# Taking the unread matrix products out of the norms' and the experts' waits

## The chip, the cores and the metric

The kernel runs on one core of one Trainium2 chip. The metric is the device time of one execution in microseconds (us). A core has a matrix engine (TensorE, PE in the rows, whose weight loads are shown apart as PEld), a vector engine (VectorE, DVE), a scalar engine (ScalarE, ACT), GpSimd (POOL) and SyncE (SP), which issues the loads. Each runs its own instruction stream, and they wait for each other through semaphores. Matrix products go into eight accumulator banks (PSUM). The profile also tells which share of TensorE's full clock was granted: 1.00 is 2.4 GHz and 0.50 is 1.2 GHz.

## The reference

Three transformer blocks in fp32 on x of 256 rows by 1024 columns. Cut to its structure:

```python
def reference(x, ...):
    # first block
    x = x + hybrid_mixer(rmsnorm(x), ...)                       # gated delta rule and mLSTM
    x = x + memory_cross_attention(rmsnorm(x), rmsnorm(mem), ...)
    x = x + peer_ffn(rmsnorm(x), ...)                           # 16384 experts, top 16 of each head
    h = rmsnorm(x, norm_final_w)
    # second block; post_norm(h, y) = layer_norm(DN_ALPHA * h + y)
    h = post_norm(h, 0.5 * swiglu(h, ...))                      # norm 0
    h = post_norm(h, chunked_sgu_mixer(h, ...))                 # norm 1
    h = post_norm(h, 0.5 * swiglu(h, ...))                      # norm 2
    shared = nsa_shared_kv(h, ...)
    h = post_norm(h, 0.5 * swiglu(h, ...))                      # norm 3
    h = post_norm(h, nsa_mixer(h, shared, ...))                 # norm 4
    return post_norm(h, 0.5 * swiglu(h, ...))                   # norm 5
```

## The kernel before

The 256 rows of x lie in two tiles of 128 rows, `k.x[:, 0, :]` and `k.x[:, 1, :]`. A product needs x with its columns on the partitions, so after each norm TensorE turns both tiles with eight 128x128 transposes each (`turn_chunks`, the transposes are line L575). ScalarE then takes the high part of each bank of four transposes (`split_high`, L404) and VectorE the low part (`split_low`, L409), since every large product is made of three passes, high by high, high by low and low by high (L398, L399, L400, and L3080, L3081 in the gated feed-forward). Weights stream through a ring of slots; ScalarE takes their high part (L247, L301) and VectorE their low part (L256, L307). The stages follow each other in the order of the program. Stages inside one `joined_stages` have no barrier between them; where one such group ends, all engines meet (lines L464 and L479 in the rows).

At the end of a stage that ends in a norm, the last products of tile 0 finish first, then those of tile 1. While TensorE still works on tile 1, VectorE and ScalarE normalise tile 0, and TensorE turns it as soon as its products are out (`norm.tensor`). Then tile 1 must be normalised: VectorE adds the banks to x, ScalarE squares and takes the root, VectorE takes the reciprocal (L2907, L2619, L2724) and scales the two halves (L2911, L2623, L2728), and TensorE turns tile 1, either at once (`last`) or as the first thing of the next stage (`turn_last`, called from `high_first`). In this interval TensorE has no product of the model to make. It runs `stand_in` there: n products of the identity by a constant into a bank that is not read. Its products are line L584. There are eight such places:

| place | where | products in `stand_in` | what comes next on TensorE |
|---|---|---|---|
| 1 | norm after the mixer (`RmsNorm`) | 4 + 6 + 4 | turning tile 1 in the joined stage |
| 2 | norm after the memory attention (`RmsNorm`) | 4 + 6 + 4 | a barrier, then turning tile 1 |
| 3 | the experts' end (`pick_and_run_experts`) | 12, turning tile 0, 8 | a barrier, then turning tile 1 |
| 4 | norm 0 (`PostNorm`) | 3 | the first product of the next stage, by tile 0 alone |
| 5 | norm 1 (`PostNorm`, `last`) | 3 + 7 + 4 | turning tile 1, then a barrier |
| 6 | norm 2 (`PostNorm`) | 3 + 7 + 4 | turning tile 1 in the joined stage |
| 7 | norm 3 (`PostNorm`, `last`) | 3 + 7 + 4 | turning tile 1, then a barrier |
| 8 | norm 4 (`PostNorm`) | 3 + 7 + 4 | turning tile 1 in the joined stage |

Between the portions TensorE waits for VectorE's sum or mean of tile 1 (`added`, `negated`) and for ScalarE's root of it (`rooted`). `turn_chunks` has its own wait for the normalised halves (`normed`). Norm 5 has no `stand_in`.

Of the kernel before, what the change touches and what calls it, by code (L numbers as in the profile page):

```python
# [27 lines left out]
P = 128  # L28
D = 1024
SEQ = 256  # L30
TILES = SEQ // P
# [536 lines left out]
def turn_chunks(pe, k, src, tile, ready, first=0, normed=None, own=range(8)):  # L568

    for c in own:
        if normed is not None and c % 4 == 0:
            pe.wait_ge(normed, 2 * tile + c // 4 + 1)
        ins = pe.transpose(k.psum[:, first + 2 * tile + c // 4, c % 4 * P:(c % 4 + 1) * P], src[:, c * P:(c + 1) * P],  # L575
                           k.ident[:, :])
        if c % 4 == 3:
            ins.then_inc(ready, 1)


def stand_in(pe, k, n, bank=1):

    for _ in range(n):
        pe.matmul(k.psum[:, bank, 0:P], k.ident[:, :], k.ones[:, :], start=True, stop=True)  # L584


def first_norm(k, ctx, begun, xn, gain):
# [1618 lines left out]
def pick_and_run_experts(k, room):  # L2206
# [8 lines left out]
    with ExitStack() as ctx, k.stage() as block:  # L2215
# [37 lines left out]
        def _(pe):  # L2253
# [97 lines left out]
            for i in range(TILES):  # L2351
                for m in (KEYS - 2, KEYS - 1):
                    pe.wait_ge(w_low, m + 1)
                    for half in range(2):
                        pe.wait_ge(tiles.low_done, 2 * (KEYS + m) + half + 1)
                        ins = v_tile(m, half, i)
                ins.then_inc(v_done, 1)
            stand_in(pe, k, 12, 7)
            turn_chunks(pe, k, k.x[:, 0, :], 0, banks, 4, normed)
            stand_in(pe, k, 8, 7)  # L2360

        @block.scalar
        def _(act):
# [294 lines left out]
class PostNorm:  # L2658
# [104 lines left out]
    def tensor(self, pe):  # L2763
        if self.begin:
            turn_chunks(pe, self.k, self.k.x[:, 0, :], 0, self.banks, 4, self.normed)
            stand_in(pe, self.k, 3)
            if self.which != 0:
                pe.wait_ge(self.negated, 2 * TILES)
                stand_in(pe, self.k, 7)
                pe.wait_ge(self.rooted, 2)  # L2770
                stand_in(pe, self.k, 4)
            if self.last:
                self.turn_last(pe, range(DC))

# [96 lines left out]
class RmsNorm:  # L2871
# [72 lines left out]

    def tensor(self, pe):
        turn_chunks(pe, self.k, self.rows[0], 0, self.banks, 4, self.normed)
        stand_in(pe, self.k, 4)
        pe.wait_ge(self.added, 2)
        stand_in(pe, self.k, 6)
        pe.wait_ge(self.rooted, 2)  # L2950
        stand_in(pe, self.k, 4)

    def ends(self):

# [1223 lines left out]
```

## Time and profile before

| what | value |
|---|---|
| time, median of 3 runs | 2253.13 us (2252.58 to 2254.63) |
| the profiled execution's own time | 2254.57 us |
| its span, first to last instruction | 2252.0 us |
| TensorE busy | 2198.6 us, 98% of the span |
| VectorE busy | 1585.8 us, 70% |
| ScalarE busy | 1170.2 us, 52% |
| mean granted clock of TensorE | 0.994 |
| products of `stand_in` | 107 |

The profiled execution has 2.57 us outside its span. Busy time of TensorE is modelled at its ends, so 98% says that it has nearly always something in hand, not that it runs at its peak.

### The profile page before, as it was taken

The page shows a single profiled execution, that of the slowest core. Times are in us where ns is not written, and L with a number is a line of the kernel's source. Part 1 is how long each engine was busy: PE and PEld are TensorE (multiplying, and loading weights), DVE is VectorE, ACT ScalarE, POOL GpSimd, SP SyncE. Part 2 cuts the span into 40 slices and gives each one's busy share as a digit, 9 for nine tenths or more (in the row PEclk, how much of TensorE's full clock was granted, in tenths as well). Part 3 has the DMA queues.
Part 4 walks back from the last instruction along what each step waited for, and adds up shares of the span by engine and source line. Part 5 has one row for each costly group of instructions (what it writes and reads, how often), then busy time and mean ns, then how long its engine had stood idle before and what let it go on. Part 6 is the DMA issues. An engine that isn't in the chain of part 4 may idle for free. (4 is left out here: it accounts for less than half of the span.)

```text
span 2252.0 us, 37012 instructions
## 1 busy us (share of the span) xinstructions
PE 2198.6 (98%) x14606; PEld 1964.1 (87%) x14606; DVE 1585.8 (70%) x2838; ACT 1170.2 (52%) x2007; POOL 38.1 (2%) x21
## 2 busy tenths in 40 slices
PE   7989999999999999999999999999999999999998
PEld 7977889999999998888888889988889788878887
DVE  7975659998889976666666657765657565786655
ACT  6543444555554455565555545544544554585444
POOL 0101000110000000000000000000000000000000
PEclk9999999999999999999999999999999999999999
DMA  7418424555444456656656556536555655404552
GB/s 272 150 45 187 169 86 162 175 175 173 147 146 149 144 170 193 195 192 193 195 183 218 180 195 234 197 127 225 174 203 190 251 179 202 165 30 169 187 200 99
DMA packets 78308, 389.95 MB, mean 173 GB/s; under 512 B 9771, under 2 KB 12715, under 8 KB 49868
## 3 DMA queue, kind: packets, MB, share of 16 engines
q1 hardware_dynamic: 76684, 383.33, 49.2%
q0 software_dynamic: 1040, 4.19, 1.5%
q8 instruction: 105, 1.72, 0.3%
q14 instruction: 47, 0.39, 0.1%
q10 hardware_dynamic: 432, 0.33, 0.0%
HBM read 382.57 MB, written 5.24 MB: 172 GB/s over the span
## 5 line engine op out<-in xcount | busy, mean ns | idle before, releaser
L256 DVE TENSOR_TENSOR split_slots<-ring,split_slots 128x1024 fp32r<-128x1024 f32 x402 | 476.6, 1230 | 116.6 <-ACT split_slots L247 116.4
L247 ACT ACTIVATE split_slots<-ring 128x1024 fp32r<-128x1024 f32 x402 | 402.4, 1054 | 154.3 <-PE banks L400 133.4
L3080 PE MATMUL banks<-x_transposed,split_slots 128*128 128x512 f32 x1360 | 479.9, 396 | 2.0 <-PEq L464 2.0
L409 DVE SCALAR_TENSOR_TENSOR expert_lo<-ring,expert_hi 128x512 fp32r<-128x512 f32 x512 | 362.3, 713 | 165.6 <-ACT expert_hi L404 164.4
L404 ACT ACTIVATE expert_hi<-ring 128x512 fp32r<-128x512 f32 x512 | 324.0, 634 | 259.9 <-PE banks L400 259.9
L3081 PE MATMUL banks<-x_transposed,split_slots 128*128 128x256 f32 x1360 | 382.2, 281 | 0.0
L3080 PEld LDWEIGHTS banks<-x_transposed,split_slots 128*128 128x128 f32 x1360 | 256.1, 188 | 62.4 <-issue 2.2
L398 PE MATMUL banks<-x_transposed,expert_hi 128*128 128x256 f32 x1024 | 294.7, 288 | 6.5 <-DVE expert_lo L409 6.5
L399 PE MATMUL banks<-x_transposed,expert_hi 128*128 128x256 f32 x1024 | 288.5, 282 | 0.0
L400 PE MATMUL banks<-x_transposed,expert_lo 128*128 128x256 f32 x1024 | 288.5, 282 | 0.0
L3081 PEld LDWEIGHTS banks<-x_transposed,split_slots 128*128 128x128 f32 x1360 | 257.1, 189 | 1.5
L3179 DVE TENSOR_TENSOR gate_and_value<-banks,products_with_low_parts 128x512 f32<-128x512 f32 x88 | 60.8, 691 | 201.9 <-ACT products_with_low_parts L3135 201.9
L398 PEld LDWEIGHTS banks<-x_transposed,expert_hi 128*128 128x128 f32 x1024 | 193.9, 189 | 8.1 <-issue 4.5
L400 PE MATMUL banks<-expert_hi,weighted_split 128*128 128x512 f32 x512 | 199.2, 389 | 0.0
L399 PE MATMUL banks<-expert_lo,weighted_split 128*128 128x512 f32 x512 | 199.2, 389 | 0.0
L398 PE MATMUL banks<-expert_hi,weighted_split 128*128 128x512 f32 x512 | 199.2, 389 | 0.0
L400 PEld LDWEIGHTS banks<-x_transposed,expert_lo 128*128 128x128 f32 x1024 | 193.8, 189 | 0.0
L399 PEld LDWEIGHTS banks<-x_transposed,expert_hi 128*128 128x128 f32 x1024 | 193.8, 189 | 0.0
L3135 ACT ACTIVATE products_with_low_parts<-banks 128x512 f32<-128x512 f32 x88 | 52.7, 598 | 244.2 <-PE banks L3081 239.0
L398 PE MATMUL banks<-x_transposed,split_slots 128*128 128x256 f32 x544 | 154.8, 285 | 2.3 <-PEq L464 2.0
L399 PE MATMUL banks<-x_transposed,split_slots 128*128 128x256 f32 x544 | 153.5, 282 | 0.0
L400 PE MATMUL banks<-x_transposed,split_slots 128*128 128x256 f32 x544 | 153.4, 282 | 0.0
(489 smaller groups left out, 4026.3 us busy)
## 6 DMA issues: line engine op xcount, KB each, us to landing
ring<-in_ffn_w SPq DMA_DIRECT2D x132, 1024.0 KB, 4.8
ring<-in_peer_u SPq DMA_DIRECT2D x128, 512.0 KB, 3.5
ring<-in_peer_v SPq DMA_DIRECT2D x128, 512.0 KB, 4.2
ring<-in_w_in SPq DMA_DIRECT2D x16, 1024.0 KB, 5.2
ring<-in_sgu_w_in SPq DMA_DIRECT2D x16, 1024.0 KB, 4.8
ring<-in_peer_wq SPq DMA_DIRECT2D x8, 1024.0 KB, 6.1
ring<-in_sgu_w_out SPq DMA_DIRECT2D x8, 1024.0 KB, 4.8
ring<-in_kv_w SPq DMA_DIRECT2D x6, 1024.0 KB, 4.8
```

What stands on the lines that cost most here:

```text
L247: act.activation(self.parts[:, b, 0, p], self.k.w.slot(g)[:, p], ACT.Copy).then_inc(self.high_done, 1)
L256: ins = dve.tensor_tensor(self.parts[:, b, 1, p], self.k.w.slot(g)[:, p], self.parts[:, b, 0, p].bitcast(F32), ALU.subtract)
L398: pe.matmul(out, lh, rh, start=start, stop=False)
L399: pe.matmul(out, lh, rl, start=False, stop=False)
L400: return pe.matmul(out, ll, rh, start=False, stop=stop)
L404: return act.activation(dst, src, ACT.Copy, scale=scale)
L409: return dve.scalar_tensor_tensor(dst, src, scale, hi.bitcast(F32), ALU.mult, ALU.subtract)
L3080: pe.matmul(out(j, slice(0, 2 * SEQ)), lh, k.xT.both[:, c, :, :], start=(c == 0), stop=False)
L3081: ins = pe.matmul(out(j), ll, rh, start=False, stop=(c == DC - 1))
L3135: act.activation(rest[:, n, :, :], sums(u, n, 1), ACT.Copy).then_inc(copied[n], 1)
L3179: dve.tensor_tensor(whole[:, n, :, :], sums(u, n, 0), rest[:, n, :, :], ALU.add).then_inc(joined[n], 1)
```

## The change

All calls of `stand_in` go, and so does the function. In `PostNorm.tensor` TensorE's waits for `negated` and `rooted` go with them. In `RmsNorm.tensor` its waits for `added` and `rooted` stay, with no product between or behind them in that method. The transposes, their own waits and all else are as before.

```diff
-def stand_in(pe, k, n, bank=1):
-    for _ in range(n):
-        pe.matmul(k.psum[:, bank, 0:P], k.ident[:, :], k.ones[:, :], start=True, stop=True)
@@ pick_and_run_experts, tensor
                 ins.then_inc(v_done, 1)
-            stand_in(pe, k, 12, 7)
             turn_chunks(pe, k, k.x[:, 0, :], 0, banks, 4, normed)
-            stand_in(pe, k, 8, 7)
@@ PostNorm.tensor
             turn_chunks(pe, self.k, self.k.x[:, 0, :], 0, self.banks, 4, self.normed)
-            stand_in(pe, self.k, 3)
-            if self.which != 0:
-                pe.wait_ge(self.negated, 2 * TILES)
-                stand_in(pe, self.k, 7)
-                pe.wait_ge(self.rooted, 2)
-                stand_in(pe, self.k, 4)
             if self.last:
                 self.turn_last(pe, range(DC))
@@ RmsNorm.tensor
         turn_chunks(pe, self.k, self.rows[0], 0, self.banks, 4, self.normed)
-        stand_in(pe, self.k, 4)
         pe.wait_ge(self.added, 2)
-        stand_in(pe, self.k, 6)
         pe.wait_ge(self.rooted, 2)
-        stand_in(pe, self.k, 4)
```

## Rows read from the trace of the kernel before

**Rows 1.** The page: busy time of each engine.
```profile
PE 2198.6 (98%) x14606; PEld 1964.1 (87%) x14606; DVE 1585.8 (70%) x2838; ACT 1170.2 (52%) x2007; POOL 38.1 (2%) x21
```

**Rows 2.** Line L584: durations in ns (least, median, most), first and last start.
```profile
L584 PE MATMUL banks<-ones,ident x214: 272/275/377, 261.5 to 2059.2; 128*128 128x128 f32 x107
```

**Rows 3.** Timeline of PE, seven ends of gaps: start, us, what, [idle before <-releaser].
```profile
122.33 0.70 PE L1404 MATMUL banks<-gc_diagonal,constants_sb 128*128 128x512 f32 x1 [1.78 <-DVE gc_diagonal L1303]
...
151.66 0.55 PE L398 MATMUL banks<-memory_T,x_transposed 128*128 128x256 f32 x1 [1.59 <-PEq L479]
...
390.82 0.39 PE L398 MATMUL banks<-x_transposed,expert_hi 128*128 128x256 f32 x1 [1.56 <-DVE expert_lo L409]
...
400.51 0.36 PE L398 MATMUL banks<-x_transposed,expert_hi 128*128 128x256 f32 x1 [3.75 <-DVE expert_lo L409]
...
1177.23 1.06 PE L575 MATMUL banks<-ident,x_natural 128*128 128x128 f32 x8 [1.56 <-PEq L479]
...
1516.40 0.47 PE L3080 MATMUL banks<-x_transposed,split_slots 128*128 128x512 f32 x1 [2.00 <-PEq L464]
...
1953.74 0.43 PE L398 MATMUL banks<-x_transposed,split_slots 128*128 128x256 f32 x1 [2.00 <-PEq L464]
```

**Rows 4.** Windows of PE: stretch, length, busy (matmuls), granted clock, DMA share, GB/s.
```profile
151.63:155.04 3.41, 3.38 (x16) 0.50 0.15 37
400.81:404.22 3.41, 3.41 (x18) 0.50 0.46 150
...
1179.05:1182.46 3.41, 3.41 (x19) 0.50 1.02 334
1182.46:1185.87 3.41, 3.41 (x31) 1.00 0.96 372
1516.97:1520.38 3.41, 3.41 (x13) 0.50 0.86 256
1520.38:1523.79 3.41, 3.41 (x21) 1.00 1.04 412
1953.87:1957.28 3.41, 3.41 (x17) 0.50 0.69 239
1957.28:1960.69 3.41, 3.41 (x31) 1.00 0.86 311
```

**Rows 5.** Timeline of PE at places 1, 2, 3 and 8.
```profile
261.51 3.29 PE L584 MATMUL banks<-ones,ident 128*128 128x128 f32 x28
264.70 1.23 PE L575 MATMUL banks<-ident,normed_rows 128*128 128x128 f32 x8
...
329.85 3.29 PE L584 MATMUL banks<-ones,ident 128*128 128x128 f32 x28
334.48 1.07 PE L575 MATMUL banks<-ident,first_blocks 128*128 128x128 f32 x8 [1.34 <-PEq L464]
...
1170.17 2.84 PE L584 MATMUL banks<-ones,ident 128*128 128x128 f32 x24
1172.85 1.04 PE L575 MATMUL banks<-ident,x_natural 128*128 128x128 f32 x8
1173.72 1.95 PE L584 MATMUL banks<-ones,ident 128*128 128x128 f32 x16
...
2055.78 3.74 PE L584 MATMUL banks<-ones,ident 128*128 128x128 f32 x28
2059.51 1.22 PE L575 MATMUL banks<-ident,x_natural 128*128 128x128 f32 x8
```

**Rows 6.** Timeline of DVE at places 3, 5 and 8.
```profile
1171.70 1.42 DVE L2623 SCALAR_TENSOR_TENSOR x_natural<-x_natural,final_stats,final_gain 128x512 f32<-128x512 f32 x2
...
1175.70 1.22 DVE L307 TENSOR_TENSOR split_slots<-ring,split_slots 128x1024 fp32r<-128x1024 f32 x1
...
1513.60 2.47 DVE L409 SCALAR_TENSOR_TENSOR x_transposed<-banks,x_transposed 128x512 fp32r<-128x512 f32 x4
...
2058.61 1.41 DVE L2728 SCALAR_TENSOR_TENSOR x_natural<-banks,norm_stats,norm_gain_bias 128x512 f32<-128x512 f32 x2
```

## Prediction

> **What bounds the kernel now.** I read the page first. TensorE is busy for 98% of the span, VectorE for 70% and ScalarE for 52% [rows 1]. So what TensorE has to issue sets the time, and a change counts only by what it does to TensorE: what it issues, what it waits for, and its clock. The mean granted clock of 0.994 in the table above can hide short losses, so I asked for the clock of single stretches.
>
> Next I read line L584, the only one that the change takes out. It has 214 matmuls, two for each of 107 products [rows 2].
>
> Third, the timeline of TensorE at the eight places [rows 5]. At place 1 the 28 matmuls start at 261.51 and the next transposes at 264.70, so 3.19 us are filled without a break, 0.114 us a matmul. The same holds at place 2. At place 8 the fill is 3.73 us, with the short wait for the mean inside. Places 5, 6 and 7 have the same 28 matmuls and the same shape as place 8. Place 4 has only 6 matmuls.
>
> Last, the ends of gaps that the kernel already has, and the clock just behind them. They carry the argument.
>
> | gap ends | gap, us | full clock lost behind it |
> |---|---|---|
> | 400.51 | 3.75 | yes, from 400.81 |
> | 1516.40 | 2.00 | yes, from 1516.97 |
> | 1953.74 | 2.00 | yes, from 1953.87 |
> | 151.66 | 1.59 | yes, from 151.63 |
> | 1177.23 | 1.56 | yes, from 1179.05 |
> | 122.33 | 1.78 | no |
> | 390.82 | 1.56 | no |
>
> The gaps are in [rows 3] and the slow stretches in [rows 4]. For the two last rows of the table no stretch at 0.50 follows. A gap of 1.34 us at place 2 [rows 5] is not followed by one either. So near 1.6 us it goes both ways, and each of the three gaps of 2 us or more shown here was followed by a stretch at 0.50, that is at 1.2 GHz.
>
> **The change part by part.** *The products themselves.* 107 products of 0.228 us are 24.4 us of TensorE's time. They give back almost nothing, since all of them stand in front of something that is late for another reason. At place 8 VectorE's two scalings start at 2058.61 and take 1.41 us together, so the first half is out at 2059.3 [rows 6]. The transposes start at 2059.51 [rows 5]. Of these 0.2 us some is the wait's own, so the products hold them up by 0 to 0.2 us, and I take 0.1. At place 3 the first half of tile 0 is out at about 1172.4 [rows 6] and the transposes start at 1172.85 [rows 5], 0.4 us late. There VectorE, which doesn't need the transposes, goes on until 1175.70 + 1.22 = 1176.9 [rows 6]. The barrier behind it lets the next transposes start at 1177.23 [rows 3]. So the 0.4 us is covered. Without that cover it would be a gain of 0.4. I take 0.1 us for each of places 1, 6 and 8, and nothing at 2, 3, 5 and 7, which end in a barrier. At place 5 VectorE takes low parts until 1513.60 + 2.47 = 1516.1 [rows 6], just ahead of TensorE's next product at 1516.40 [rows 3], so it is VectorE that reaches the barrier last. I read 2 and 7, of the same build, in the same way. At place 4 the next product waits for ScalarE. Gain: 0.3 us, with bounds of 0 and 0.8.
>
> *The waits taken out.* The transposes behind them wait for the normalised halves, which come later than the mean and the root. Nothing else is queued between. Cost and gain: nothing. If those waits were late the transposes would start sooner, and this lies in the bound of 0.8.
>
> *The gaps.* Where L584 stood, TensorE is now idle. Less the modelled tail of the last transpose (0.17 us), the gap is 3.0 us at place 1 and 3.6 us at places 5 to 8. At place 2 it runs from 330.0 to 334.48, 4.5 us, since the old 1.34 us joins it. At place 3 a gap of 2.3 us comes before the transposes of tile 0 and one of 3.3 us after them. Places 5 and 7 keep their gap of 2.00 us behind the transposes of tile 1. Place 4 gets 0.7 us, which by the table is too short, so it costs nothing. By the table, I expect the clock to fall to 0.50 at all seven others.
>
> *The price of a slow stretch.* The three pairs of [rows 4] have the same length, 3.41 us. At 0.50 TensorE got through 19, 13 and 17 matmuls and at 1.00 through 31, 21 and 31. That is 12 of 31, 8 of 21 and 14 of 31 missing, or 1.3, 1.3 and 1.5 us. The counts include matmuls cut by the edges, so this is a lower end. Half of the stretch, 1.7 us, is the upper end. I take 1.5 us where a stretch lies on products for its whole length.
>
> The Trainium skill (TensorE: Matmul & The Clock Gate, section Terms) puts the penalty at the throttled time multiplied by 1 − K/N. By it a stretch would cost 1.7 us, and the four new ones below up to 6.8 us.
>
> The same page (section HAM oscillation — how this bites in real kernels) speaks against this change: when a wait separates bursts of products, each burst starts throttled again. [...]
>
> *Where the stretch falls.* In [rows 3, 4] it begins between 0.57 us after the end of a gap of 2.00 us and, at 1953.87, only 2.1 us after such a gap had begun. A longer gap can therefore take the first part of the slow stretch into itself, where it costs nothing. At places 6 and 8 (gap 3.6 us) it can begin 1.5 us before the gap's end, and 1.9 us of it lie on products: 0.85 us. The other end is 1.5 us. I take the middle, 1.2 us each. At place 1 (3.0 us) the same gives 1.1 to 1.5, and I take 1.3. At place 2 (4.5 us) it gives 0.5 to 1.5, and I take 1.0. Sum for the new ones: 1.2 + 1.2 + 1.3 + 1.0 = 4.7 us.
>
> *Places 3, 5 and 7.* The profiled execution already loses its clock here once, behind the last gap, so that is no new cost against it. New is a fall before the transposes. Eight transposes at half clock take about 0.9 us longer than the 0.87 us of now. The second four wait for VectorE's second half anyway, and at place 5 VectorE's four low parts fill 2.47 us up to the barrier [rows 6], so a late bank delays only the last of them. I bound it by 0 and 0.9 us for each place and take 0.4 at 5 and 7 and 0.1 at 3, where VectorE sets the barrier with weights: 0.9 us.
>
> *Sum.* 4.7 + 0.9 − 0.3 = +5.3 us. Against the profiled execution's own 2254.57 us (span 2252.0 and 2.57 around it) this gives 2259.9 us. That execution is 1.44 us above the median of the runs, about one slow stretch. If the median execution had one stretch less at the gaps near 1.6 to 2 us, the longer gaps make it certain now, and the result is the same 2259.9. If the difference has another cause, it is 2253.13 + 5.3 = 2258.4. I take 2259.3 us, nearer the first.
>
> **The rivals.**
>
> *The clock holds.* TensorE keeps its full clock over most of the new gaps. For it: gaps of 1.78 and 1.56 us left no trace [rows 3], and the work on either side of the new gaps is dense. Against it: each new gap but one is 2.3 us or more, longer than the two of 2.00 us, which both lost it. Only place 2, the longest, would then fall: 2253.13 − 0.3 + 1.0 = 2253.8 us, within 0.2%. With none it is 2252.8. It decides if fewer than four places show a new stretch at 0.50.
>
> *The unread products hold up the transposes.* This ends on the other side. TensorE works through L584 while the normalised half is ready, so each place starts late. The rows bear out 0.1 us at place 8 and 0.4 at place 3. If 0.4 were on the path at all eight places, 3.2 us would come back: 2249.9 us. That is still within 0.2%. To be faster by over 0.2% it takes 0.56 us at each place, which the rows at place 8 exclude unless VectorE or ScalarE also become faster when TensorE is still. It also needs the clock to hold.
>
> *The slow level stays longer.* After a long idle time with thin work around it, the level of 0.50 could last for two such stretches at places 1, 2, 6 and 8, since the first part lies on transposes that wait for halves. Against it: in all five cases of [rows 4] the clock is seen at 0.50 for one stretch, and the three pairs show 1.00 right behind it. Price: four times 1.5 us more, 2259.3 + 6.0 = 2265.3 us.
>
> **How the numbers follow.** Forecast as above: 0.71. The clock holds: 0.17. The unread products hold up the transposes: 0.03. The slow level stays longer: 0.09. A difference of 0.2%, 4.5 us, is about what a measurement of this kernel can tell from no change, so the borders are 2248.6 and 2257.6. Of the forecast's 0.71, 0.03 may fall below 2257.6, by the low bounds of the prices. Slower: 0.68 + 0.09 = 0.77. Same: 0.03 + 0.17 + 0.01 = 0.21. Faster: 0.02.
>
> For the range the terms' low ends are 0.85 + 0.85 + 1.1 + 0.5 + 0 − 0.8 = +2.5, and the high ends 4 × 1.5 + 3 × 0.9 = +8.7. Against the median 2253.13 that is 2255.6 to 2261.8, and against the profiled execution 2257.1 to 2263.3. I take 2255.8 to 2262.8. It leaves out most of the first two rivals and the third.
>
> **What the profile after would show.** L584 is gone. At places 1, 2, 5, 6, 7 and 8 TensorE is idle for 3.0 to 4.5 us, and the transposes start at most 0.2 us sooner after the product before than now. If I am right, stretches at 0.50 begin within or just behind those gaps, four more than now at places 1, 2, 6 and 8, and some transposes at 3, 5 and 7 start 0.21 us apart. The products outside those stretches keep their durations. VectorE's and ScalarE's steps in the norms do too. The prediction is wrong if the clock reads 1.00 behind gaps of 3 us, if the slow stretches lie wholly inside the gaps and cost nothing, or if the barrier at places 2, 3, 5 and 7 moves by more than 0.9 us.

## The result and the profile after

| | median of 5 runs | lowest to highest | profiled execution | its span |
|---|---|---|---|---|
| before | 2252.85 us | 2252.36 to 2254.63 | 2254.57 us | 2252.0 us |
| after | 2263.50 us | 2261.88 to 2264.34 | 2264.34 us | 2261.8 us |

The ratio is 1.0045, with a 95% interval of 1.0030 to 1.0059: 10.6 us slower. The forecast was slower by 6.2 us, with a range up to 2262.8 us. The sign was right, and the size was too small.

The page of the kernel after first, the row that answers to [rows 1]. TensorE is busy for 12.5 us less in a span that is 9.8 us longer.

```profile
PE 2186.1 (97%) x14392; PEld 1950.8 (86%) x14392; DVE 1586.8 (70%) x2838; ACT 1169.8 (52%) x2007; POOL 38.2 (2%) x21
```

Next the timeline of TensorE after, the products that end gaps. They answer to [rows 3, 5].

```profile
266.14 1.68 PE L575 MATMUL banks<-ident,normed_rows 128*128 128x128 f32 x8 [3.02 <-DVE normed_rows L2897]
...
337.10 0.45 PE L575 MATMUL banks<-ident,first_blocks 128*128 128x128 f32 x1 [4.46 <-PEq L464]
...
395.21 0.39 PE L398 MATMUL banks<-x_transposed,expert_hi 128*128 128x256 f32 x1 [1.57 <-DVE expert_lo L409]
...
404.90 0.55 PE L398 MATMUL banks<-x_transposed,expert_hi 128*128 128x256 f32 x1 [3.75 <-DVE expert_lo L409]
...
1177.71 1.78 PE L575 MATMUL banks<-ident,x_natural 128*128 128x128 f32 x8 [2.17 <-DVE x_natural L2615]
1182.44 0.87 PE L575 MATMUL banks<-ident,x_natural 128*128 128x128 f32 x3 [2.94 <-PEq L479]
...
1518.97 1.77 PE L575 MATMUL banks<-ident,x_natural 128*128 128x128 f32 x8 [3.59 <-DVE x_natural L2720]
1522.43 0.77 PE L3063 MATMUL banks<-x_transposed,split_slots 128*128 128x512 f32 x1 [1.68 <-PEq L464]
...
1713.73 0.43 PE L575 MATMUL banks<-ident,x_natural 128*128 128x128 f32 x2 [3.66 <-DVE x_natural L2720]
...
1957.82 1.97 PE L575 MATMUL banks<-ident,x_natural 128*128 128x128 f32 x8 [3.56 <-DVE x_natural L2720]
1961.47 0.55 PE L398 MATMUL banks<-x_transposed,split_slots 128*128 128x256 f32 x1 [1.68 <-PEq L464]
...
2067.97 0.30 PE L575 MATMUL banks<-ident,x_natural 128*128 128x128 f32 x1 [3.59 <-DVE x_natural L2720]
```

In brackets stands the idle time before a product. The gaps are where they were expected and within 0.1 us of the expected length, but for the two at place 3 (2.17 and 2.94 us for 2.3 and 3.3) and the ones behind the transposes at places 5 and 7 (1.68 for 2.00). Then the windows over each stretch at 0.50 behind them: stretch, length, busy (matmuls), granted clock, DMA share, GB/s. They answer to [rows 4].

```profile
335.00:341.83 6.83, 4.73 (x22) 0.50 0.46 178
403.27:410.10 6.83, 5.20 (x24) 0.50 0.39 128
1178.10:1188.34 10.24, 7.30 (x34) 0.50 0.64 246
1519.43:1526.26 6.83, 5.15 (x18) 0.50 0.42 110
1956.34:1966.58 10.24, 7.08 (x32) 0.50 0.40 133
266.74:270.15 3.41, 3.41 (x17) 0.50 0.02 5
1713.99:1717.40 3.41, 3.41 (x17) 0.50 0.20 43
2068.98:2072.39 3.41, 3.32 (x16) 0.50 0.79 267
```

At places 1, 6 and 8 the clock is lost for 3.41 us. At places 2 and 5 it is lost for 6.83 us, and at 3 and 7 for 10.24. In all of [rows 4] it was 3.41. The stretch at 403.27 is the one that began at 400.81 before. Its gap of 3.75 us has not changed, but it now lasts 6.83 us.

What each place cost comes from how much later the same product starts than before:

| between | shift before it | shift behind it | cost, us |
|---|---|---|---|
| start, up to place 1 | 0 | 266.14 − 264.70 = 1.44 | 1.44 |
| place 1 | 1.44 | 337.10 − 334.48 = 2.62 | 1.18 |
| place 2 | 2.62 | 395.21 − 390.82 = 4.39 | 1.77 |
| the experts' gap of 3.75 us | 4.39 | 1182.44 − 1177.23 = 5.21 | 0.82 |
| places 3 and 4 | 5.21 | 1518.97 − 1513.09 = 5.88 | 0.67 |
| place 5 | 5.88 | 1713.73 − 1707.48 = 6.25 | 0.37 |
| place 6 | 6.25 | 1957.82 − 1950.42 = 7.40 | 1.15 |
| place 7 | 7.40 | 2067.97 − 2059.51 = 8.46 | 1.06 |
| place 8 | 8.46 | 2261.8 − 2252.0 = 9.8 | 1.34 |

The starts at 1513.09, 1707.48 and 1950.42 are those of the same transposes in the timeline of before. The eight places sum to 7.54 us; place 4 adds nothing to its row (the products are 5.95 us late ahead of it, at 1190, and 5.89 behind it, at 1508). Outside them are 0.82 us at the experts and 1.44 us at the start.

The 1.44 us at the start are a matter of the clock too, though the column of the granted clock doesn't say so: its record begins with the first change to 1.00, and a window before that reads 1.00 whatever the clock is. Until 20.98 products of 256 columns start 0.213 us apart in the kernel after. In the kernel before they are 0.117 apart from 18.51 on.

### The profile page after: what moved, and what is told of

It reads as the page before. It is cut to its first block and busy times, and to the rows that moved or that the text cites. A ratio compares the mean times of both kernels' runs of the same rounds, so it can differ in the third digit from the quotient of the medians.

```text
span 2261.8 us, 36588 instructions
## 1 busy us (share of the span) xinstructions
PE 2186.1 (97%) x14392; PEld 1950.8 (86%) x14392; DVE 1586.8 (70%) x2838; ACT 1169.8 (52%) x2007; POOL 38.2 (2%) x21
```

## The experiments

Each ratio is against the kernel before on the same chip. The first four kernels shared one chip (median before 2251.54 us), the next four another (2253.47), the last two another (2252.63). The median of before thus moves by 2 us between chips.

**1. Only the places with no barrier behind them.** The unread products go at places 1, 6 and 8 and stay at the others.

```diff
 PostNorm.tensor:
-            stand_in(pe, self.k, 3)
-            if self.which != 0:
-                ...
+            if self.which in (0, 1, 3):
+                (the same lines)
 RmsNorm.tensor:
+        if not self.same:
+            (the same lines)
```

> The unread products are taken out only at places 1, 6 and 8, where no barrier follows, and stay at 2, 3, 4, 5 and 7. Theory (the clock): in the profile of the changed kernel the products behind these three places are late by about 1.2 us (1), 0.8 us (6) and 1.4 us (8), each with one stretch at 0.50. So this kernel should be 3.4 us above the kernel before, with three stretches at 0.50 more. Rival (the slow level that lasts longer, at the places with a barrier, carries nearly all of the 10.6 us): under 1.5 us. Rival (idle TensorE costs something of its own, whatever the clock): the shift appears with the clock at 1.00.

Measured: 2256.57 us (11 runs), ratio 1.0020 [1.0011, 1.0029], 5.0 us slower, where 3.4 was expected. Windows of its profile, the three stretches at 0.50 that are new, and two that are at 1.00 where [rows 4] has 0.50:

```profile
264.65:268.06 3.41, 3.29 (x15) 0.50 0.00 0
1182.00:1185.00 3.00, 3.00 (x28) 1.00 1.02 373
1708.49:1711.90 3.41, 3.41 (x15) 0.50 0.22 48
1956.00:1959.00 3.00, 3.00 (x26) 1.00 0.67 216
2060.06:2066.89 6.83, 5.79 (x26) 0.50 0.61 200
```

The clock is lost at all three places, and there the products are late by 1.2 us (1), 1.2 us (6) and 2.2 us (8). Place 8 lost 6.83 us of full clock here and 3.41 in the kernel after. At places 3 and 7, whose code is that of before, this execution kept the clock and gained 1.5 and 0.6 us on the profiled execution of before. So with the same code at the place the clock falls behind a gap of 1.6 to 2 us in one execution and not in another. The stretch behind the experts' gap lasts 6.83 us here too and costs 1.2 us. The terms 1.2 + 1.2 + 2.2 + 1.2 − 1.5 − 0.6 give 3.7 of the 3.8 us between the two profiled executions.

**2. Only the places with a barrier behind them.** The reverse: the products go at 2, 3, 5 and 7 and stay at 1, 4, 6 and 8.

```diff
 PostNorm.tensor:
+            if self.which not in (1, 3):
+                (the same lines)
 RmsNorm.tensor:
+        if self.same:
+            (the same lines)
 pick_and_run_experts:
-            stand_in(pe, k, 12, 7)
-            stand_in(pe, k, 8, 7)
```

> The unread products are taken out only at places 2, 3, 5 and 7, where a barrier follows, and stay at 1, 4, 6 and 8. Theory (the clock, with a level of 0.50 that lasts for two or three stretches of 3.41 us here): the shifts in the profile of the changed kernel are 1.8, 0.7, 0.6 and 1.0 us against an execution of before that already had three stretches here, so 4.1 us above such an execution, and up to 7 us above the median of before, if the median execution has them more seldom. With the joined places alone it should add up to the 10.6 us of the whole change. Rival (the price per place is that of the prediction, 1.0 + 0.9 us): about 2 us.

Measured: 2260.82 us, ratio 1.0037 [1.0023, 1.0051], 9.3 us slower, above the 4.1 to 7 us expected. Windows of its profile:

```profile
334.02:340.85 6.83, 5.55 (x25) 0.50 0.64 228
1177.12:1187.36 10.24, 7.29 (x33) 0.50 0.66 241
1518.45:1525.28 6.83, 5.15 (x17) 0.50 0.43 118
1955.35:1965.59 10.24, 8.00 (x36) 0.50 0.42 148
2062.00:2072.00 10.00, 9.66 (x80) 1.00 0.41 134
```

The same long stretches as in the kernel after, and none at place 8. This rules out the price of the prediction, 2 us, for these four. The two halves sum to 14.3 us by the medians, more than the 10.6 of the whole. Their intervals, 2.5 to 6.5 and 5.2 to 11.5 us, allow for it. By the profiled executions they sum to 3.8 + 6.9 = 10.7 us, but that they agree so well with 9.8 or 10.6 is luck: the 3.8 are what is left after 2.1 us that experiment 1's execution gained where nothing was changed, the 6.9 hold 0.8 us lost at the start, and each holds the experts' loss (1.2 and 1.0 us), which comes once in the whole change.

**3. The instruction stream without the work.** Each unread product becomes three whose result is 16 by 16.

```diff
-    for _ in range(n):
-        pe.matmul(k.psum[:, bank, 0:P], k.ident[:, :], k.ones[:, :], start=True, stop=True)
+    for _ in range(3 * n):
+        pe.matmul(k.psum[0:16, bank, 0:16], k.ident[:, 0:16], k.ones[:, 0:16], start=True, stop=True)
```

> All unread products stay in their places, but each is replaced by three of 16 columns by 16 in place of one of 128 by 128. The stream of instructions on TensorE goes on through the waits, with one sixty-fourth of the elements in each. Theory (the clock follows how much the array does, not whether an instruction is there): stretches at 0.50 at the same places as without any, and 8 to 11 us above the kernel before. Rival (it is an empty queue or the waking from a wait that costs): as the kernel before, within 1 us.

Measured: 2260.77 us, ratio 1.0035 [1.0021, 1.0048], 9.2 us slower. The line of the products in the profile (durations in ns), then windows, the first one behind place 1:

```profile
L584 PE MATMUL banks<-ones,ident x642: 176/176/190, 259.7 to 2062.7; 128*16 128x16 f32 x161
```

```profile
264.00:267.41 3.41, 3.23 (x28) 1.00 0.00 0
333.78:337.19 3.41, 3.30 (x15) 0.50 0.94 322
1176.88:1183.71 6.83, 6.03 (x28) 0.50 0.74 251
1514.79:1521.62 6.83, 5.15 (x19) 0.50 0.41 108
1955.11:1961.94 6.83, 5.24 (x24) 0.50 0.58 200
```

642 matmuls run in the waits, three times as many as before, and the clock falls at five of the eight places all the same (2, 3, 5, 7 and 6, the last from 1709.35 to 1712.76). "At the same places as without any" was a miss for places 1 and 8. By the medians the time is 9.2 us above before, against 10.6 for the kernel after, and the interval of 4.7 to 10.8 us holds both. So instructions in the queue are not enough, and the rival of an empty queue, which forecast the time of before within 1 us, is out. The profile says more: at places 1 and 8, where the clock stays at 1.00, the products behind are not later by 0.1 us, and at place 6, where it falls, they are 1.15 us later, with the same instructions in the wait. The cost goes with the clock.

What makes the clock fall here is less certain. The tiny products leave three idle pieces in each wait, 0.35, 0.39 and 0.39 us at place 6, where before had one of 0.23. I take it to be the missing work, since no gap under 1.56 us was followed by a stretch at 0.50 in the kernel before. A run with tiny products and without these pieces was not made.

**4. More unread products than before.** The gaps ahead of the barriers are filled as well.

```diff
             if self.last:
                 self.turn_last(pe, range(DC))
+                stand_in(pe, self.k, 7)
 RmsNorm.tensor, at its end:
+        if not self.same:
+            stand_in(pe, self.k, 4)
 pick_and_run_experts:
-            stand_in(pe, k, 8, 7)
+            stand_in(pe, k, 13, 7)
```

> The kernel before with more unread products where it still has gaps ahead of a barrier: 4 more at place 2, 5 more at place 3, and 7 more behind the transposes of tile 1 at places 5 and 7. Theory (the clock): the profiled execution of before lost its clock behind the gaps at places 3, 5 and 7, 1.5 us each. With these gaps filled it should keep 1.00 there, and be 1.5 to 4.5 us faster than that execution, 0 to 3 us faster than the median of before, since there the clock may have been lost more seldom. Rival (those gaps do not set the time, or the products delay the barrier): same or up to 1 us slower.

Measured: 2251.17 us, ratio 0.9997 [0.9988, 1.0006], no difference in the medians. Windows of its profile behind the experts' gap, where nothing was added, and at places 3, 5 and 7:

```profile
401.18:404.59 3.41, 3.41 (x18) 0.50 0.50 151
1174.00:1184.00 10.00, 9.31 (x80) 1.00 0.66 233
1514.00:1524.00 10.00, 9.56 (x57) 1.00 0.80 292
1950.00:1960.00 10.00, 8.85 (x74) 1.00 0.72 271
```

The three stretches at places 3, 5 and 7 are gone, and this execution (2251.19 us) is 3.4 us faster than the profiled one of before. The products behind places 3, 5 and 7 come 1.54, 1.52 and 0.62 us sooner. At place 7 a part of what the clock gives back is lost again: 6 us later, at 1957.69, TensorE waits 0.71 us for VectorE's `narrow_split`, and in before it has no wait there. Its 11 runs lie between 2250.34 and 2253.52 us, those of before between 2249.35 and 2254.21. The gain against the one execution is the theory's. By the medians, 0.4 us apart, theory and rival can't be told from each other.

**5. The kernel after, once more.**

> The changed kernel once more, on the chip of this group, with a second profile. Theory (the clock): again stretches at 0.50 at places 1, 2, 3, 5, 6, 7 and 8, those at places 2, 3, 5 and 7 mostly for more than one stretch of 3.41 us, in another pattern than the first profile, and 9 to 11.5 us above the kernel before. Where the clock stays at 1.00 in both profiles, the distances between the same products are the same within 0.1 us. Rival (the first profile was unlucky, the usual price is the 6 us of the prediction): under 8 us.

Measured: 2263.32 us, ratio 1.0045 [1.0032, 1.0059], the same as at first. Windows of the second profile:

```profile
333.59:340.42 6.83, 4.51 (x21) 0.50 0.46 164
401.85:408.68 6.83, 5.09 (x24) 0.50 0.36 121
1176.68:1186.92 10.24, 7.30 (x34) 0.50 0.65 238
1954.92:1965.16 10.24, 7.23 (x33) 0.50 0.37 130
```

The pattern did not change, against what I expected: each stretch has the same length as in the first profile, the one at place 5 (6.83 us from 1518.01) as well. The places cost nearly the same too: 1.1 (1), 1.7 (2), 0.7 (3 and 4), 0.0 (5), 1.2 (6), 1.1 (7) and 1.4 us (8), and the experts' gap 0.75. At the start this execution (2262.92 us) is only 0.3 us later than the first one of before. So the 1.44 us there belong to the first execution and not to the change. The profiles of experiments 2 and 7 also have the first full clock only at 20.00 and 20.54, by chance as well, since nothing is changed there.

**6. The kernel before, once more.**

> The kernel before once more, for a second profile. The first one was 2 us above the median and lost its clock behind places 3, 5 and 7. Theory: an execution near the median of before lost its clock at one or two of these three less, 1.5 us each. So if this one takes 2251 to 2252 us, one or two of the stretches at 1179, 1517 and 1954 are missing in it. Rival: all three are there whatever the time, and the difference lies elsewhere.

Measured: 2254.82 us, with all three stretches, at 1179, 1517 and 1954, and no shift over 0.1 us across any of the places (it runs 0.2 to 0.4 us late between them). It was again an execution near the top of the range (21 runs of before on this chip took 2251.14 to 2254.83 us), so it doesn't tell what a faster one does. Experiment 1 does, in part: in it two of the three stretches were missing. The mean granted clocks of the 21 runs say the rest: the five at 0.994 took 2254.46 to 2254.83 us, the ten at 0.996 took 2251.14 to 2253.90, with a median of 2252.2. A stretch of 3.41 us at 0.50 takes 3.41 × 0.5 / 2252 = 0.0008 off the mean, so by this estimate the ten had two or three such stretches less. Which ones isn't seen.

**7. Only the last four products.** Those behind the root stay.

```diff
 PostNorm.tensor:
-            stand_in(pe, self.k, 3)
             if self.which != 0:
-                pe.wait_ge(self.negated, 2 * TILES)
-                stand_in(pe, self.k, 7)
                 pe.wait_ge(self.rooted, 2)
                 stand_in(pe, self.k, 4)
 (RmsNorm.tensor the same; 4 and 4 in place of 12 and 8 at the experts' end)
```

> Only the last 4 of the 14 unread products stay, those behind the root of tile 1, at places 1, 2, 5, 6, 7 and 8; 4 and 4 stay of the 12 and 8 at place 3, none of the 3 at place 4. TensorE is idle for about 2.3 us less the wait for the root in front of them, in place of 3.6. Theory (the clock goes by how long TensorE has been idle in the last few us): it still falls behind most of these places, but for shorter: 4 to 7 us above before. Rival (what counts is that products run right before the transposes): within 1.5 us of before.

Measured: 2257.19 us (11 runs), ratio 1.0017 [1.0008, 1.0026], 3.7 us slower, a little under the 4 to 7 of the theory and above the rival's 1.5 (the interval is 1.8 to 5.9 us). Two of the six stretches in its profile:

```profile
334.57:337.98 3.41, 3.02 (x13) 0.50 0.01 2
1181.08:1184.49 3.41, 3.07 (x14) 0.50 0.57 150
```

The clock still falls at six of the seven places, but each time for 3.41 us alone. That four products run right before the transposes doesn't keep the clock. It does shorten the stretches at the places with a barrier. (The experts' stretch lasts 6.83 us here as well.)

**8. Filling the other gaps.** On top of experiment 4:

```diff
 gdn_prepare:
             ins.then_inc(w_done, 1)
+            stand_in(pe, k, 6, 2)
 pick_and_run_experts:
             for m in range(KEYS):
+                if m in (0, 2):
+                    stand_in(pe, k, 6 if m == 0 else 15, 0)
                 u_products(m)
```

> The kernel with more unread products at places 2, 3, 5 and 7, and in addition 6 at the end of the stage that prepares the delta rule (the gap of 1.59 us that ends at 151.66), and 6 and 15 in front of the first and the third of the experts' products (the gaps of 1.56 and 3.75 us that end at 390.82 and 400.51). Theory (the clock): the stretches at 151.6 and 400.8 go too, 1.5 us each, so 2 to 3 us faster than the run with the first addition alone, 2 to 4 us faster than before. Rival (products in front of the experts' delay them as much as the clock gives back): same as before within 1 us.

Measured: 2249.00 us (11 runs), ratio 0.9981 [0.9972, 0.9990], 4.5 us faster than before. Windows of its profile, where [rows 4] has 0.50:

```profile
151.00:161.00 10.00, 9.70 (x72) 1.00 0.36 138
400.00:410.00 10.00, 10.00 (x86) 1.00 0.64 208
```

The products behind the two gaps come 1.3 and 1.5 us sooner. Against its own profiled execution (2248.2 us) that of before is 6.4 us slower: 1.3 + 1.5 + 1.5 + 1.5 + 0.6.

**9. Unread products only behind the transposes.** The kernel after, with 13 products at place 3 and 7 at places 5 and 7, in the second gap, and none in the first.

```diff
 against the kernel after:
             if self.last:
                 self.turn_last(pe, range(DC))
+                stand_in(pe, self.k, 7)
 pick_and_run_experts, behind turn_chunks:
+            stand_in(pe, k, 13, 7)
```

> The changed kernel, so nothing runs in the wait for tile 1 at places 1, 2, 4, 6 and 8. Only where a second gap follows a first set of transposes unread products are put behind these: 13 at place 3 (before the barrier), 7 at places 5 and 7 (behind the transposes of tile 1, before the barrier). Theory A (the slow level lasts for 6.8 or 10.2 us there because a second gap follows the first while the clock is already down): with the second gap filled, places 5 and 7 show a stretch of 3.4 us, place 3 at most 6.8, and the kernel is 1 to 3 us faster than the changed one, so 7 to 9 us above before. Theory B (the length comes from the first gap of 3.6 us alone): the stretches stay at 6.8 to 10.2 us and the time stays within 1 us of the changed kernel, 9 to 11 us above before.

Measured: 2263.26 us, ratio 1.0048 [1.0034, 1.0061], 10.6 us slower: no gain over the kernel after. Windows of its profile at places 2, 3, 5 and 7, then the second gap at place 5:

```profile
335.90:339.31 3.41, 3.41 (x18) 0.50 0.77 247
1175.58:1178.99 3.41, 3.41 (x18) 0.50 0.54 226
1516.91:1520.32 3.41, 3.41 (x17) 0.50 0.00 0
1953.81:1960.64 6.83, 5.71 (x25) 0.50 0.00 0
```

```profile
1517.14 3.19 PE L584 MATMUL banks<-ones,ident 128*128 128x128 f32 x14
1520.63 0.47 PE L3071 MATMUL banks<-x_transposed,split_slots 128*128 128x512 f32 x1 [0.30 <-PEq L464]
```

The stretches at 3, 5 and 7 together fall from 27.3 to 13.7 us. That is theory A's side for their length, except at place 7. Place 2 warns that this isn't all: its code is that of the kernel after, and its stretch fell from 6.83 to 3.41 us too. Here it begins 0.50 us behind the end of the gap, in the three other profiles of this code 1.27 to 2.33 us ahead of it.

Theory A's gain in the time did not come: the median did not move. The rows show a reason. The unread products run at the low clock themselves (at place 5, 14 matmuls in 3.19 us, where 28 take 3.29 us at place 1 in before) and hold up the barrier: behind it the first product comes 1.2, 1.3 and 1.6 us later than in the kernel after, at places 3, 5 and 7, each measured from the work ahead of its place. That takes back most of what the clock gives. This profiled execution took 2261.57 us, the lowest but one of the five runs. The slower ones were not seen.

**10. The start as well.** Experiment 8 and

```diff
 first_norm, behind the transposes:
+        for _ in range(10):
+            pe.matmul(k.psum[:, 0, 0:P], k.ident[:, :], k.ident[:, :], start=True, stop=True)
```

> The fastest version so far, and 10 products of the identity by itself behind the very first transposes, in the gap of 2.62 us that ends at 14.75. Theory (the clock): the last stretch at 0.50 in the middle of the kernel, at 15.5, goes, 1.5 us faster than the version without it, 5 to 6.5 us faster than before. Rival (the clock isn't up yet at the start in some executions, so that nothing can be kept): the same as the version without it within 0.5 us, 4.5 us faster than before.

Measured: 2247.80 us (11 runs), ratio 0.9978 [0.9969, 0.9987], 4.8 us faster than before, where the theory had 5 to 6.5 and the rival 4.5. It is the fastest version, though its interval overlaps with that of experiment 8. Windows of its profile:

```profile
15.00:25.00 10.00, 10.00 (x86) 1.00 0.88 346
120.90:124.31 3.41, 3.27 (x26) 0.50 0.00 0
```

The stretch at 15 is gone, and one shows at 120.90, around the end of the gap of 1.78 us (at 121.04) that left no trace before. That the added products took the stretch at 15 away isn't shown: the profile of experiment 3, with nothing added at the start, has none there either, and one at 122.16.

## Why the prediction was right in sign and wrong in size

**Right: the products themselves give nothing back.** The prediction took 0.1 us for each of places 1, 6 and 8. The transposes there start less than 0.02 us sooner after the product before, so it is nothing. At place 3 they start 5.21 − (1177.71 − 1172.85) = 0.35 us sooner by the shift of 5.21, and the barrier took it, as the prediction had it. The rival of held-up transposes is out.

**Right: the clock falls at seven places and not at place 4.** The gaps measured 3.02, 4.46, 2.17 and 2.94, 3.59, 3.66, 3.56 and 3.59 us. The rival of a clock that holds is out. Experiments 3, 4 and 8 show that the time goes with the clock.

**Right in price: places 1, 6 and 8.** Taken at 1.3, 1.2 and 1.2 us less 0.1 each, measured 1.18, 1.15 and 1.34. At place 8 the fit has some luck in it: the same wait cost 2.2 us in experiment 1, where the stretch began 1.03 us ahead of the gap's end and lasted 6.83 us. In the kernel after it begins 1.0 us behind it.

**Wrong: that one stretch of 3.41 us follows at places 2, 3, 5 and 7, whatever of it lies in the gap.** This is the step that failed: "A longer gap can therefore take the first part of the slow stretch into itself, where it costs nothing", and with it the length taken from "in all five cases of [rows 4] the clock is seen at 0.50 for one stretch". In those five the stretch begins at or behind the end of its gap, and dense products are on it. (At 1179.05 it begins 1.8 us behind, later than the 0.57 us that the prediction gave as the latest. Its upper price of 1.5 us covers that.) Two things were not like that after the change.

- At place 2 the stretch begins inside the gap of 4.46 us, 2.10 us ahead of its end. It doesn't end sooner for that. It lasts 6.83 us, also in experiments 5 (2.33 us ahead) and 2 (1.27). In experiment 9, with the same code there, it begins behind the end, lasts 3.41 us and costs 1.1 us in place of 1.77.
- At places 3, 5 and 7 eight transposes, a second gap and a barrier follow the first gap while the clock is low. The level stayed for 10.24, 6.83 and 10.24 us, in three profiles out of three (after, experiments 2 and 5). With the second gap filled it lasted 3.41 us at 3 and 5. At 7, where it begins 0.8 us inside the first gap, it lasted 6.83 (experiment 9).

The terms: place 2 was taken at 1.0 and measured 1.77, place 3 at 0.1 and measured 0.67 (place 4 adds nothing), place 7 at 0.4 and measured 1.06. Place 5 was taken at 0.4 and measured 0.37. Together 1.9 against 3.87 us. The rival of a level that stays longer named the mechanism, and its 2265.3 us is nearer to the 2263.5 measured than the forecast's 2259.3. But it put the long level at 1, 2, 6 and 8, where only place 2 shows it, and had a chance of only 0.09.

**Wrong by omission: a gap that the change doesn't touch.** The experts' gap of 3.75 us cost 0.82 us more, and no term of the sum stands for it. Its stretch now begins 1.6 us before the gap's end and lasts 6.83 us, where it began 0.3 us behind the end and lasted 3.41. Over the ten profiles in which this gap isn't filled the two go together without exception. In seven (after, experiments 1, 2, 3, 5, 7 and 9) the stretch begins 0.65 to 1.82 us ahead of the gap's end and lasts 6.83 us. In three (before, experiments 4 and 6) it begins 0.05 to 0.37 us behind it and lasts 3.41. That the shift of its start causes this is my reading. No run moved the start alone.

**The median.** Sum of the profile: 5.3 forecast, 2.24 more at the places, 0.82 at the experts and 1.44 at the start give the 9.8 us measured. The start is chance of one execution, as experiment 5 shows. In the medians something else fills its room: 10.65 us on the first chip and 9.85 on the second. Profiled executions of before were near the top of its range both times, 1.7 and 1.35 us above the median, while those of after were 0.8 above and 0.4 below. The prediction took 2259.3 us, "nearer the first" of its two sums, as if the missing stretches of the median would be the only difference. That a median execution of before has fewer stretches than the profiled one is borne out by the mean clocks in experiment 6. At which gaps was not seen.

## What to carry to other kernels

A product that nobody reads can pay for itself: where TensorE waits between dense stretches, ask for the granted clock of the few microseconds behind the wait, not for the mean over the span (0.994 here, against 0.987). In this kernel empty waits of 3 us and more lost the clock in every profile, and those of 1.56 to 2.00 us in some. Price such a wait by where the stretch begins and by what follows it: 0.6 to 1.5 us where it begins at or behind the wait's end and dense products follow, up to 2.2 us where it begins inside the wait, and more than one stretch where thin work, a second wait and a barrier follow. Once the sum of such terms is made, ask also which other gaps move in time, since they can be priced anew. Put unread products into the whole of the wait: put only behind it they ran at the low clock and held up the barrier (experiment 9).

## What the hardware showed that I had not expected

**The lost clock can last longer than in the rows before.** Lengths were 3.41, 6.83 and 10.24 us. Dense products alone don't end it at once: at place 7 after they run from 1961.47, and the level of 0.50 lasts until 1966.58.

**Half the clock costs less than half of the rate.** Products of 256 columns start every 0.213 us at 0.50 and every 0.117 us at 1.00, a factor of 1.82 where the clocks differ by 2. Timeline of the kernel after at place 1, at 0.50:

```profile
268.11 0.42 PE L356 MATMUL banks<-x_transposed,split_slots 128*128 128x256 f32 x1
268.32 0.41 PE L359 MATMUL banks<-x_transposed,split_slots 128*128 128x256 f32 x1
268.54 0.41 PE L356 MATMUL banks<-x_transposed,split_slots 128*128 128x256 f32 x1
```

So 3.41 us at 0.50 lose 3.41 × (1 − 0.117 / 0.213) = 1.54 us. Experiment 4 measured 1.54 and 1.52 us for such a stretch at places 3 and 5 (and 0.62 at place 7, where a wait of 0.71 us for VectorE took most of the rest). The Trainium skill (TensorE: Matmul & The Clock Gate, section Terms) puts the penalty at the throttled time multiplied by 1 − K/N, an estimate of 3.41 × 0.5 = 1.7 us. This case's runs stay below it.

**Instructions in the queue don't hold the clock.** 42 tiny products in a wait of 3 to 4 us didn't hold it at five places of eight (experiment 3). The products of full size held it in both profiles of the kernel before, but for the gaps that they leave at places 3, 5 and 7.
